# Output-weight staging in the last phase of a two-layer hybrid trunk: two raw buffers in place of five

## The reference

```
def _hybrid_layer(x, ...):
    h = _rmsnorm(x, norm_g)
    proj = h @ w_in
    ...
    y_swa = _swa_attention(_heads(sq), _heads(sk), _heads(sv), swa_sinks, swa_q_norm, swa_k_norm, pos)
    y_conv = _short_conv(cb, cc, cx, conv_w)
    mixed = jnp.concatenate([y_fox * jax.nn.silu(fg), y_rwkv * jax.nn.silu(rg),
                             y_swa * jax.nn.silu(sg), y_conv * jax.nn.silu(cg)], axis=-1)
    return x + mixed @ w_out
```

## Time and profile before

| | us |
|---|---|
| median of 3 runs | 3691.14 |
| lowest and highest | 3688.15, 3694.39 |
| the profiled execution's own time | 3691.14 |
| its span, first to last instruction | 3689.3 |
| TensorE busy in the span | 3284.0 (89%) |
| VectorE busy | 1552.2 (42%) |
| ScalarE busy | 1009.4 (27%) |
| GpSimd busy | 545.5 (15%) |

### The profile page before, as it was taken

One profiled execution on the slowest core, in us unless ns is written; L12 is line 12 of the kernel. 1 busy time (PEld: TensorE's weight loads), 2 busy tenths in 40 slices (PEclk: granted clock), 3 DMA queues, 4 the chain that ended last, 5 costly groups with the idle time before them and its releaser, 6 DMA issues. The chain is left out here.

```text
span 3689.3 us, 62205 instructions
## 1 busy us (share of the span) xinstructions
PE 3284.0 (89%) x24708; PEld 2331.3 (63%) x24708; DVE 1552.2 (42%) x2258; ACT 1009.4 (27%) x1876; POOL 545.5 (15%) x304
## 2 busy tenths in 40 slices
PE   6979989999997688959979799899999976889599
PEld 4868767777774344437748687677777743444387
DVE  4127622222223565557441376222222235655575
ACT  4014312222223134333240143122222231343332
POOL 4100000000000112332241000000000001122322
PEclk9989999999998578979979899899999985788799
DMA  3225422222223310066332254222222233100663
GB/s 118 74 70 174 142 74 66 80 66 65 64 66 120 116 29 18 9 187 209 120 110 74 70 174 144 73 64 80 68 65 64 66 120 116 29 18 9 187 203 123
DMA packets 357723, 343.29 MB, mean 93 GB/s; under 512 B 95388, under 2 KB 290972, under 8 KB 353592
## 3 DMA queue, kind: packets, MB, share of 16 engines
q1 hardware_dynamic: 288520, 298.53, 25.5%
q10 hardware_dynamic: 68928, 40.93, 4.2%
HBM read 208.46 MB, written 130.91 MB: 92 GB/s over the span
## 5 line engine op out<-in xcount | busy, mean ns | idle before, releaser
L124 PE MATMUL rs_acc<-h_hi,rs_w_hi 128*128 128x512 f32 x1024 | 428.4, 418 | 0.0
L128 PE MATMUL rs_acc<-h_lo,rs_w_hi 128*128 128x512 f32 x1024 | 417.8, 408 | 0.0
L130 PE MATMUL rs_acc<-h_hi,rs_w_lo 128*128 128x512 f32 x1024 | 414.5, 405 | 0.0
L110 POOL TENSOR_TENSOR rs_w_lo<-rs_raw,rs_w_hi 128x1024 fp32r<-128x1024 f32 x32 | 76.3, 2386 | 1235.8 <-POOLq L109 1235.8
L124 PE MATMUL rp_acc<-h_hi,rp_w_hi 128*128 128x512 f32 x512 | 206.0, 402 | 41.7 <-PEq L121 41.7
L1372 ACT ACTIVATE fx_prob<-fx_ST 128x512 f32<-128x512 f32 (+3 forms) x320 | 157.2, 531 | 290.7 <-PE fx_ST L1242 150.8
L1658 PE MATMUL so_acc<-so_wo_hi,so_m_hi 128*128 128x512 f32 x512 | 209.3, 409 | 29.9 <-POOL so_m_lo L1580 25.2
L124 PEld LDWEIGHTS rs_acc<-h_hi,rs_w_hi 128*128 128x128 f32 x1024 | 192.2, 188 | 55.1 <-issue 16.5
L130 PEld LDWEIGHTS rs_acc<-h_hi,rs_w_lo 128*128 128x128 f32 x1024 | 192.6, 188 | 43.2
L128 PEld LDWEIGHTS rs_acc<-h_lo,rs_w_hi 128*128 128x128 f32 x1024 | 192.7, 188 | 36.7
L124 PE MATMUL pj_acc<-h_hi,pj_w_hi 128*128 128x512 f32 (+1 forms) x512 | 207.4, 405 | 5.3 <-PEq L121 5.3
(11 more groups left out here) (256 smaller groups left out, 6006.6 us busy)
## 6 DMA issues: line engine op xcount, KB each, us to landing
projT<-rs_stage SPq DMA_DIRECT2D x128, 256.0 KB, 2.1
pj_xb<-x SPq DMA_DIRECT2D x32, 512.0 KB, 3.3
projT<-rp_stage SPq DMA_DIRECT2D x64, 256.0 KB, 3.1
rs_raw<-w_in ACTq DMA_DIRECT2D x32, 512.0 KB
rs_nat<-rw SPq DMA_DIRECT2D x128, 128.0 KB, 2.4
so_stage<-x SPq DMA_DIRECT2D x64, 256.0 KB, 2.9
rp_pre<-projT SPq DMA_DIRECT2D x16, 899.5 KB, 8.3
projT<-pj_stage SPq DMA_DIRECT2D x56, 256.0 KB, 2.0
```

Source lines behind the costliest of these rows:

```text
L110: self.nc.gpsimd.tensor_tensor(self.w_lo[q][:, :, 0:m], self.raw[:, :, 0:m], self.w_hi[q][:, :, 0:m].bitcast(F32), ALU.subtract).then_inc( ...
L124: ins = M(acc, self.w_hi[q][:, k, 0:m], self.h_hi[:, k, cols], start=(k == 0), stop=False)
L128: M(acc, self.w_hi[q][:, k, 0:m], self.h_lo[:, k, cols], start=False, stop=False)
L130: ins = M(acc, self.w_lo[q][:, k, 0:m], self.h_hi[:, k, cols], start=False, stop=(k == KC - 1))
```

## The change

Two raw buffers take the place of five, and one semaphore per buffer takes the place of one per slice. `load_weights(i)` waits for the subtraction of slice i - 2, and the requests are spread between the splits. On VectorE `weights(0)` moves behind `gates`, and `weights(2)` behind `mixed`.

```
-        NW = 5
-        raw = [P.sb(f"raw{i}", [128, DM]) for i in range(NW)]
+        raw = [P.sb(f"raw{e}", [128, DM]) for e in two]
...
-        w_in = [P.sem(f"w_in{c}") for c in range(KC)]
...
             def load_weights(i):
-                c = KO[i]
-                if i >= NW:
-                    act.wait_ge(s["wlo_p" if by_pool(i - NW) else "wlo_d"], (i - NW) // 2 + 1)
+                kk, e = KO[i], i % 2
+                if i > 1:
+                    act.wait_ge(s["wlo_p" if by_pool(i - 2) else "wlo_d"], (i - 2) // 2 + 1)
...
             def split(i):
-                c = KO[i]
-                act.wait_ge(w_in[c], 32 if c in (4, 5) else 16)
-                A(wo_hi[:, c, :], raw[i % NW][:], ACT.Copy).then_inc(s["whi_rdy"], 1)
+                got[i % 2] += 32 if KO[i] in (4, 5) else 16
+                act.wait_ge(raw_in[i % 2], got[i % 2])
+                A(wo_hi[:, KO[i], :], raw[i % 2][:], ACT.Copy).then_inc(s["whi_rdy"], 1)
...
-            for i in range(NW):
+            for i in two:
                 load_weights(i)
...
                     if n < 0:
-                        for i in range(3):
+                        for i in range(2):
                             split(i)
+                            load_weights(i + 2)
                     act.wait_ge(s["t_rdy"], m + 1)
...
                     if n < 0:
-                        for i in range(NW, KC):
-                            load_weights(i)
-                        for i in range(3, 6):
+                        for i in range(2, 4):
                             split(i)
+                            load_weights(i + 2)
                     for i in range(3):
                         rounded(m, i)
...
                     if n < 0:
-                        for i in range(6, KC):
+                        for i in range(4, KC):
                             split(i)
+                            if i + 2 < KC:
+                                load_weights(i + 2)
                     rounded(m, 3)
...
-                if n < 0:
-                    weights(0)
-                else:
+                if n >= 0:
                     add_x(n, 0)
                 if m < N:
                     gates(m)
                 if n < 0:
-                    weights(2)
+                    weights(0)
                 else:
                     add_x(n, 1)
                 if m < N:
                     mixed(m)
-                if n >= 0:
+                if n < 0:
+                    weights(2)
+                else:
                     add_x(n, 2)
```

More of the change, by code:

```diff
@@ L1418, in phase_swa_out @@
         s = {n: P.sem(n) for n in names}
-        a_in, g_in, y_in, cv_in = ([P.sem(f"{n}{e}") for e in two] for n in ("a_in", "g_in", "y_in", "cv_in"))
-        w_in = [P.sem(f"w_in{c}") for c in range(KC)]
+        a_in, g_in, y_in, cv_in, raw_in = ([P.sem(f"{n}{e}") for e in two] for n in ("a_in", "g_in", "y_in", "cv_in", "raw_in"))
         x_in, x_st = ([P.sem(f"{n}{d}") for d in range(NS)] for n in ("x_in", "x_st"))
@@ L1496, in load_weights @@
             def load_weights(i):
-                c = KO[i]
-                if i >= NW:
-                    act.wait_ge(s["wlo_p" if by_pool(i - NW) else "wlo_d"], (i - NW) // 2 + 1)
-                if c in (4, 5):
+                kk, e = KO[i], i % 2
+                if i > 1:
+                    act.wait_ge(s["wlo_p" if by_pool(i - 2) else "wlo_d"], (i - 2) // 2 + 1)
+                if kk in (4, 5):
                     for h in two:
-                        r = 2 * GW + 128 * h + 64 * (c - 4)
-                        act.dma_start(raw[i % NW][half[h], :], w[r:r + 64, :]).then_inc(w_in[c], 16)
-                else:
-                    act.dma_start(raw[i % NW][:], w[c * 128:(c + 1) * 128, :]).then_inc(w_in[c], 16)
+                        r = 2 * GW + 128 * h + 64 * (kk - 4)
+                        act.dma_start(raw[e][half[h]], w[r:r + 64, :]).then_inc(raw_in[e], 16)
+                else:
+                    act.dma_start(raw[e][:], w[kk * 128:(kk + 1) * 128, :]).then_inc(raw_in[e], 16)
+            got = [0, 0]
             def split(i):
-                c = KO[i]
-                act.wait_ge(w_in[c], 32 if c in (4, 5) else 16)
-                A(wo_hi[:, c, :], raw[i % NW][:], ACT.Copy).then_inc(s["whi_rdy"], 1)
+                got[i % 2] += 32 if KO[i] in (4, 5) else 16
+                act.wait_ge(raw_in[i % 2], got[i % 2])
+                A(wo_hi[:, KO[i], :], raw[i % 2][:], ACT.Copy).then_inc(s["whi_rdy"], 1)
             def exps(n):
@@ L1584, in weights @@
                 pool.wait_ge(s["whi_rdy"], i + 1)
-                G.tensor_tensor(wo_lo[:, KO[i], :], raw[i % NW][:], wo_hi[:, KO[i], :].bitcast(F32), ALU.subtract).then_inc(s["wlo_p"], 1)
+                G.tensor_tensor(wo_lo[:, KO[i], :], raw[i % 2][:], wo_hi[:, KO[i], :].bitcast(F32), ALU.subtract).then_inc(s["wlo_p"], 1)
                 pool.drain()
@@ L1758, in weights @@
                 ve.wait_ge(s["whi_rdy"], i + 1)
-                V.tensor_tensor(wo_lo[:, KO[i], :], raw[i % NW][:], wo_hi[:, KO[i], :].bitcast(F32), ALU.subtract).then_inc(s["wlo_d"], 1)
+                V.tensor_tensor(wo_lo[:, KO[i], :], raw[i % 2][:], wo_hi[:, KO[i], :].bitcast(F32), ALU.subtract).then_inc(s["wlo_d"], 1)
             maxima(0)
```

## The result

The changed kernel is slower by about 1%: 3719.49 us, inside the stated range and on the forecast side.

What follows compares the result with a forecast made beforehand. The prediction took TensorE to bound the last phase from turns(1) on; turns(1), at 1639.80 before, would start at 1653.35, 13.5 us later per layer; 2 x 13.5 = 27 us on 3691.1 us gave 3718 us, range 3707 to 3728.

Steps and rivals of the forecast that it cites:

- TensorE is bound from turns(1) on, so the phase ends as much later as turns(1) starts: Each layer's last phase: TensorE has no hole from turns(1) on; turns(1) was forecast 13.5 us later.
- The early start: Opening of the last phase: 1.57 MB less ahead of k, q, v, first matmul 4.6 us earlier.
- The chain of handovers: Ramp of the last phase: each request waits for the subtraction two slices before; last weight pair at 1650.45, before 1637.26.
- rival A: Last phase: handovers hide, two buffers suffice, only the early gain of 4.6 us per layer is left, 3682 us; chance 0.04.
- Rival B: Opening of the last phase: fewer early bytes gain nothing, 4.6 us more per layer, 3727 us; chance 0.09.
- Rival C: Late slices need 7.3 us to land: 4.0 us more per layer, last term slice 7's 1.3 us; 3726 us; chance 0.07.
- D: All small terms of the last phase at their low ends: 4.4 us less per layer, 3709 us; chance 0.12.
- The sum, 27 us: Both layers' last phases together: 2 x 13.5 us longer, added to the profiled 3691.1 us.
- slice 7's landing: End of the ramp: slice 7 shares the DMA engines with period 1's loads, taken as 6.0 us, between 4.7 and 7.3.
- the clock: TensorE: slow price for the last weight pair, 2.90 us; no hole and an unchanged 198.7 us from turns(1) on.

Runs made afterwards that it cites:

- r1: The changed kernel run again with no edit: 3723.17 us median, ratio 1.0095 to the kernel before.
- r4: Kernel before, five buffers, but only two slices requested at the start and three behind exps(0): ratio 1.0000 to the kernel before, both last phases 6.7 us shorter.
- r3: Changed kernel with each of GpSimd's four weight subtractions done twice in a row: ratio 1.0143 to the kernel before, both last phases 53.2 us longer than before.
- r7: Changed kernel with VectorE subtracting slice 0 ahead of the gates again: ratio 1.0060 to the kernel before, both last phases 24.8 us longer than before.
- r5: Changed kernel, two buffers, but SyncE instead of ScalarE requests slices 2 to 7: ratio 1.0027 to the kernel before, both last phases 8.8 us longer than before.
- r2: Changed kernel with SyncE starting period 1's loads behind the eighth split instead of the sixth: ratio 1.0061 to the kernel before, both last phases 23.4 us longer.
- r8: Kernel before, five buffers, two slices requested by ScalarE at the start, the other six by SyncE: ratio 0.9982 to the kernel before, both last phases 7.5 us shorter.

## Why the prediction was right

Point by point, layer 0:

| step, us after the phase's start | forecast | profile after |
|---|---|---|
| first so_ matmul | 7.9 | 8.35 |
| request 2 | 25.3 | 25.7 |
| split 2 starts | 31.2 | 31.8 |
| request 5 | 37.6 | 38.05 |
| request 6 | 46.0 | 46.5 |
| request 7 | 51.7 | 51.3 |
| last split starts | 58.7 | 58.9 |
| last weight pair | 63.7 | 63.9 |
| turns(1) | 66.6 | 66.6 |

- The step "TensorE is bound from turns(1) on, so the phase ends as much later as turns(1) starts": right. In the changed kernel there is no hole behind it, 200.39 of 200.39 us, and in r1 the phase of layer 0 lengthened by 13.29 us where `turns(1)` moved by 13.28.
- The early start: 4.15 us in the profile (12.50 - 8.35), forecast 4.6. r4 shows the same 4.3 us alone, so it is the bytes and not the rest of the change. Share 1.00 was the right row to go by.
- The chain of handovers: right, and shown from both sides: lengthened by 2.5 to 3.3 us per subtraction in r3, shortened by 2.3 us in r7, and 50 to 70% of the loss gone when ScalarE doesn't wait in r5.
- That layer 0 agrees to 0.3 us at every one of the last three steps is in part luck, because errors cancelled. I misread a row: the 4.16 us of four half requests at 1616.62 are not 4 x 1.04 us. They hold a wait of 1.85 us, from 1617.79 to 1619.64, for VectorE's subtraction of slice 2, which frees slice 7's buffer; a half request takes 0.57 us at the median in both kernels. ScalarE thus stood for 5.3 us before split 3 already, not only for the 3.5 us that rival A names. So two of them take 1.18 us and not 2.1 us. Against that, the early start was 0.45 us smaller, GpSimd's first subtraction took 2.81 us beside the gated pieces and not 2.48, and slice 7 took longer than the 6.0 us I gave it.
- Rival A (two buffers suffice) is refuted: the last low part was ready at about 62.4 us, not at the 46.0 (1632.7) from which A decides. The advice of the Trainium skill ("Trainium Kernel Development and Optimization", section "Best Practices") is to double-buffer so that DMA and compute overlap. The trace agrees for the transfers of slices 2 to 6, none of which ended a split's wait. But two buffers were not enough: the splits waited for a buffer to be freed, and by r5 50 to 70% of the loss came from ScalarE's standing in that wait.
- Rival B (no early gain) is refuted by the first matmul and by r4. Rival C came true in its last term only, as its text had it. D isn't what happened; its terms, 4.4 us per layer, also add up to 8.8 us and not to the 9.1 us given.
- The sum, 27 us, was too small: the profile gives 31.6 us in the two phases. The mis-sized term is slice 7's landing, in layer 1: its halves landed after 8.5 us at the median, not 6.0, and the last split came at 61.8 us there, 3.0 us later than I priced it by taking the layers alike; r2 takes most of that away, and r1 shows that it differs between executions. The second is the clock: I let the transposes run at full speed, but in layer 0 `turns(1)` was still at the lower clock: it came 13.6 us later after the phase's start (66.64 - 53.08), but the phase got 15.0 us longer. 27 + 3.0 + 1.5 is 31.5 us. The other 1.1 us of the spans' difference lie outside the phases, within what identical code varies there.
- The time itself, 3718 us forecast and 3719.49 us measured, agrees better than the sum does, and that is luck. The forecast started from a median of 3691.14 us, which with more runs of the kernel before became 3686.08 us; the change was 33 us by the medians and 35 us by the ratio, not 27.

## What to carry to other kernels

In this kernel the smaller ring cost little by its landings as long as each was covered. Most of the cost came from the engine on which the request stands, because a request that waits for a consumer holds up everything behind it in that engine's order. So look for who frees the buffer, what stands ahead of that instruction on its engine, and issue waiting requests from a queue that has nothing else to do; what is left then is the late request itself, some 15 us here (r5 against r4). Order opening transfers by who needs them first: a deferred megabyte and a half let TensorE start 4 us earlier, of which 3.4 us per layer reached the end of the phase. And split a merged row before you price one instruction from it: a wait can lie inside it, as in the four half requests.

## What the runs showed of the hardware

- VectorE and GpSimd held each other up when both worked on two inputs in SBUF. Four fused operations of VectorE took 1.83 us alone, 3.77 us beside one GpSimd subtraction of 2.48 us and 5.91 us beside two. GpSimd's subtraction took 2.34 us alone and 2.81 us beside VectorE's gated pieces. The Trainium skill, page "SBUF — State Buffer", section "SBUF: two separate sides", says that the port pair which the two share is an exclusive lock: where VectorE's operation has two inputs in SBUF and GpSimd's reads SBUF, whichever starts first holds it for the whole instruction and the other waits. The trace agrees: each GpSimd subtraction of 2.36 to 2.48 us adds about 2 us.
- Half slices landed after 4.0 us on quiet queues, and after 6.6 and 8.5 us beside period 1's loads. Issuing one took ScalarE 0.57 us at the median (0.47 to 0.62), a whole slice over 128 partitions 0.34 us.
- The attention phase (fx_) of layer 1, which no run here changes, took 319.8 us in r4's profile and 345.8 us in r8's, with the same 1080 TensorE instructions; the granted clock was 0.83 in the one and 0.76 in the other, where full speed is 1.00 (2.4 GHz) and the lower level 0.50 (1.2 GHz). Rows of busy time by stretch, r4 first:

```profile
3097.20:3417.00 319.80, 262.20 (x1080) 132.02 (x1080) 173.11 (x190) 123.65 (x241) 87.19 (x58) 0.83 0.09 28
```

```profile
3094.60:3440.40 345.80, 289.68 (x1080) 145.15 (x1080) 171.46 (x190) 124.91 (x241) 85.33 (x58) 0.76 0.08 26
```

That is 26 us for identical code, as much as the change itself, and it may be why medians of the kernel before wander between 3686.08 and 3695.11 us. Why the clock was granted less in one run stays open; no run here separates it. For a question about one phase, that phase's length in the profile was the better measure, with the 2.6 us in mind by which it differed between two profiles of the changed kernel.
